# Splitting six output panels of a recurrent block ahead, and beginning them in six PSUM banks before its last channel tile is ready

## The reference

```python
def rglru_mixer(hx, hc, w_in, conv_w, conv_b, gate_w, gate_b, lam, w_out, need_ctx_out):
    ux = hx @ w_in
    gx, rx = ux[..., :D_RNN], ux[..., D_RNN:]            # D_RNN = 1280
    ...
    rx = centred_dwconv(rx, conv_w, conv_b)
    for d in range(2):                                   # two directions
        ax, bx = rglru_coeffs(rx, gate_w[d], gate_b[d], lam[d])
        ...                                              # h_x = linear_scan(ax, bx, h_c[:, -1])
    yx = (jax.nn.gelu(gx) * (hs_x[0] + hs_x[1]).astype(gx.dtype)) @ w_out
...
x = x + mx[:, :, 5] * yx
```

## Time and profile before

| | |
|---|---|
| median of 3 runs | 2760.24 us (2759.57 to 2760.76) |
| the profiled execution: its time, its span | 2758.28 us, 2756.5 us |
| PE, PEld busy | 2653.8 us (96%), 2476.4 us (90%) |
| DVE, ACT, POOL busy | 1428.3 us (52%), 763.1 us (28%), 895.8 us (32%) |
| DMA: moved, mean | 309.32 MB, 112 GB/s |
| granted PE clock over the span | 0.985 of full |

### The profile page before, as it was taken

How to read it: one execution, slowest core, us unless ns; L and a number is a source line. 1 busy time by engine, 2 the same in 40 slices (tenths; PEclk the granted TensorE clock), 3 DMA queues, 4 the chain that set the end, 5 groups by cost and what they waited for, 6 DMA issues and landing times.

```text
span 2756.5 us, 40602 instructions
## 1 busy us (share of the span) xinstructions
PE 2653.8 (96%) x15151; PEld 2476.4 (90%) x15151; DVE 1428.3 (52%) x2489; ACT 763.1 (28%) x1034; POOL 895.8 (32%) x418
## 2 busy tenths in 40 slices
PE   6999999999999899999999999999999997899998
PEld 5999999998968899999999899999998985778887
DVE  6666466565463666546666423422226995532233
ACT  4111122212164322111112322111114884332222
POOL 1332232322323232322222455545530002344442
PEclk9999999999999999999999999999999998999999
DMA  6443343423311243433442455545513442233332
GB/s 216 145 122 117 97 122 122 129 80 79 106 33 31 77 122 122 125 104 118 122 121 79 122 164 168 168 126 158 162 42 107 153 135 63 62 96 102 91 101 82
DMA packets 439330, 309.32 MB, mean 112 GB/s; under 512 B 9853, under 2 KB 414166, under 8 KB 439254
## 3 DMA queue, kind: packets, MB, share of 16 engines
q1 hardware_dynamic: 439254, 308.32, 36.7%
HBM read 278.92 MB, written 30.46 MB: 112 GB/s over the span
## 4 chain that ended last, share of the span: by engine, by line
PE 67%; issue 19%; POOL 6%; DVE 4%; DMA 2%; ACT 1%; SPq 1%; POOLq 0%; DVEq 0%; ACTq 0%
PE pair_a L1835 30%; PE pair_b L1835 29%; POOL w_lo L809 5%; DVE ada_sums L1258 1%; DMA unit_raw<-in_rg_gate_w_dram 1%; PE pair_b L1822 1%; PE pair_b L1823 1%; PE pair_b L1824 1%; DVE h_lo L1409 1%; PE pair_c L1924 1%; PE pair_a L1822 1%; POOL unit_hi L823 1%; PE pair_a L1823 1%; PE pair_a L1824 1%; DVE work_g L1398 0%
## 5 line engine op out<-in xcount | busy, mean ns | idle before, releaser
L809 POOL TENSOR_TENSOR w_lo<-raw,w_hi 128x1024 fp32r<-128x1024 f32 (+2 forms) x271 | 739.5, 2729 | 1652.4 <-ACT w_hi L932 1652.4
L932 ACT ACTIVATE w_hi<-raw 128x1024 fp32r<-128x1024 f32 (+2 forms) x271 | 308.9, 1140 | 1144.6 <-PE pair_b L1835 660.9
L1298 DVE TENSOR_TENSOR work_g<-work_s,pair_b 128x768 f32<-128x768 f32 (+1 forms) x88 | 78.1, 887 | 664.3 <-PE pair_b L1835 502.2
L1258 DVE SCALAR_TENSOR_TENSOR ada_sums<-ada_raw,cvec,ada_sums 128x256 f32<-128x256 f32 x896 | 388.5, 506 | 0.0
L1835 PE MATMUL pair_a<-h_hi,w_hi 128*128 128x384 f32 x1296 | 335.6, 339 | 6.4 <-POOL w_lo L809 3.9
L1835 PE MATMUL pair_a<-h_lo,w_hi 128*128 128x384 f32 x1296 | 331.0, 336 | 0.0
L1835 PE MATMUL pair_a<-h_hi,w_lo 128*128 128x384 f32 x1296 | 330.7, 336 | 0.0
L1835 PE MATMUL pair_b<-h_hi,w_hi 128*128 128x384 f32 x1168 | 296.7, 334 | 0.0
L1835 PE MATMUL pair_b<-h_hi,w_lo 128*128 128x384 f32 x1168 | 296.4, 334 | 0.0
L1835 PE MATMUL pair_b<-h_lo,w_hi 128*128 128x384 f32 x1168 | 296.2, 334 | 0.0
L1835 PEld LDWEIGHTS pair_a<-h_hi,w_hi 128*128 128x128 f32 x1296 | 232.8, 189 | 16.0 <-issue 9.9
(11 more groups left out here) (314 smaller groups left out, 4352.2 us busy)
## 6 DMA issues: line engine op xcount, KB each, us to landing
raw<-in_ffn_w_gu_dram SPq DMA_DIRECT2D x176, 512.0 KB, 3.9
ada_raw<-in_ada_w_dram SPq DMA_DIRECT2D x64, 1024.0 KB, 5.1
raw<-in_ffn_w_down_dram SPq DMA_DIRECT2D x64, 704.0 KB, 4.6
unit_raw<-in_rg_w_in_dram SPq DMA_DIRECT2D x40, 256.0 KB, 3.6
ada_first<-in_ada_w_dram SPq DMA_DIRECT2D x4, 2048.0 KB, 13.3
raw<-in_ab_w_in_dram SPq DMA_DIRECT2D x16, 512.0 KB, 3.9
u_split_dram<-unit_hi SPq DMA_DIRECT2D x20, 256.0 KB, 2.0
u_split_dram<-unit_lo SPq DMA_DIRECT2D x20, 256.0 KB, 2.3
```

The costliest lines, as they stand in the source:

```text
L809: nc.gpsimd.tensor_tensor(wl[:, par, 0:kt * P], raw[:, par, 0:kt * P], wh[:, par, 0:kt * P].bitcast(F32), ALU.subtract).then_inc(split_rea ...
L932: nc.scalar.activation(wh[:, par, 0:kt * P], raw[:, par, 0:kt * P], ACT.Copy).then_inc(hi_done, 1)
L1258: step = nc.vector.scalar_tensor_tensor(out=sums[v], in0=tiles(k), scalar=c_k, in1=sums[v], op0=ALU.mult, op1=ALU.add)
L1298: nc.vector.tensor_tensor(gbuf[:, 0, 0:W], sbuf[:, 0, 0:W], up, ALU.mult)\
```

## The change

- **Units.** 15 units more: `out_unit` splits the first 6 x 128 columns of `w_out` (`AHEAD` = 6) to a new HBM tensor `out_split`. Ten of them (4 panels wide, one k-tile) go one to each pair of `gu21`, which then has three units for a pair; five (2 panels wide, two k-tiles) go in `dn21`. The two gate units that were in `dn21` move to the first pair of `gu21`.
- **Buffers.** From unit 28 on there are two high buffers (`unit_hi` and `unit_hi2`), with a store counter for each side (`pair_stored`). SP issues a unit's load before it waits for the unit before it to be split and stored (`begin_unit`, `end_unit`, `step`, `units_of`).
- **Order in `dn20` and `dn21`.** Both panel loads and, in `dn20`, `load_ada` now go before the units; POOL does a panel's `low` before the unit, not after it.
- **Recurrent end.** SP loads the split panels from `out_split` (`load_out`): panel 0 and 1 to the two weight buffers, 2 to 5 to `out_hi`, `out_lo`, which lie over `h_hi`, `h_lo` and so wait for the last `g` product. PE does tiles 0 to 7 of panel 0 before the gates of tile 9, tiles 0 to 7 of panels 1 to 5 after them, each panel in a bank of its own (`OUT_BANKS`), then tile 8 of all six, then tile 9 of all six. Panels 6 and 7 are loaded early to `raw` and split by ACT and POOL once panels 0 and 1 are through. ACT's and POOL's splits of panels 0 to 5 go.

```diff
+        unit_hi2 = at("unit_hi2", [P, UNIT], F32R, scr_at + size([P, 4, T]) + size([P, T]))
+        out_hi = at("out_w_hi", [P, AHEAD - 2, KR * P], F32R, h_at)
+        out_lo = at("out_w_lo", [P, AHEAD - 2, KR * P], F32R, h_at + size([P, KD, T]))
...
+        OUT_BANKS = [pA[:, 0:512], pB[:, 0:512], pC[:, 0:512], pA[:, 512:1024], pB[:, 512:1024], pR[:, 0:512]]
...
+        UNITS_UP = [(28, 2)] + [(30 + 3 * i, 3) for i in range(KC - 1)]
+        UNITS_DOWN = [[(20 + 2 * i, 2) for i in range(4)], [(60, 2), (62, 2), (64, 1), (65, 0)]]
...
+            def begin_unit(k, r, src, later):
+                if isinstance(k, int) and k >= PAIRED + 2:
+                    sp.wait_ge(pair_stored[r], stored_before(k))
+                elif later or isinstance(k, int) and k >= PAIRED:
+                    sp.wait_ge(unit_stored, k * 32 - 31)
+                n = src.shape[-1]
+                sp.dma_start(unit_raw[r][:, :].rearrange("p (k n) -> p k n", n=n), src).then_inc(unit_landed[r], 16)
...
+            def step(k, unit):
+                begin_unit(k, k % 2, unit[0], True)
+                finish_held()
+                held.append((k, k % 2, unit[1]))
...
+                    def gate_up_ahead(i, k, units):
+                        for r in range(2):
+                            load(i * 2 + (split_no(p0) + r), r, KD, gu[:, :, span(i * P + (r * DFF + h * KC * P), P)])
+                            step(k + r, units[r])
+                        if len(units) > 2:
+                            step(k + 2, units[2])
...
-            sp.wait_ge(unit_stored, 50 * 32 + 1)
+            sp.wait_ge(unit_stored, PAIRED * 32 + 1)
+            for r in range(2):
+                sp.wait_ge(pair_stored[r], stored_before(60 + r))
...
+            for r in range(2):
+                p = P_RGOUT + AHEAD + r
+                load(split_no(p), r, KR, wro[:, :, (AHEAD + r) * P:(AHEAD + r + 1) * P])
+            for r in range(2):
+                sp.wait_ge(pair_stored[r], stored_before(66 - r))
+            sp.wait_ge(panel_used, u_panel(KR - 1) + 1)
+            load_out(0, 0, KR, out_landed[0])
             load_gates(KR - 1)
-            with sp.Fori(0, KD // 2) as i:
-                for r in range(2):
-                    load(i * 2 + (split_no(P_RGOUT) + r), r, KR, wro[:, :, span(i * (2 * P) + r * P, P)])
+            sp.wait_ge(panel_used, g_panel(KR - 1) + 1)
+            load_out(1, 0, KD, out_landed[1])
+            for n in range(2, AHEAD):
+                load_out(n, 0, KR, out_landed[n])
+            sp.wait_ge(panel_used, gate_panel(KR - 1) + 1)
+            load_out(1, KD, KR, out_end_landed)
...
+                    if P_RGOUT + AHEAD <= p < P_RGOUT + KD:
+                        act.wait_ge(panel_used, p - AHEAD + 1)
...
-                if n == KR - 1:
-                    high(P_RGOUT)
                 gelu_rows(n)
...
-            high(P_RGOUT + 1)
+            high(P_RGOUT + AHEAD)
+            high(P_RGOUT + AHEAD + 1)
             outputs("rgout", P_RGOUT)
...
-                    pe.wait_ge(resid_done, UPD[name] + KD - 2 + r - 1)
+                    pe.wait_ge(resid_done, UPD[name] + (KD - 2 + r - 1 if name != "rgout" else 4 + r))
...
+            pe.wait_ge(out_landed[0], 32)
+            pe.wait_ge(u_done, KR)
+            out_part(0, range(KR - 2))
             pe.wait_ge(gates_done, 4 * (KR - 1))
             gates((KR - 1) % 2, KR - 1)
+            for n in range(1, AHEAD):
+                pe.wait_ge(out_landed[n], 32)
+                if n == 1:
                     pe.wait_ge(gelu_x_done, KR)
                     pe.wait_ge(gelu_q, KR)
+                else:
+                    pe.wait_ge(gates_done, 4 * (KR - 1) + (2 if n == 2 else 4))
+                out_part(n, range(KR - 2))
+            pe.wait_ge(out_end_landed, 32)
+            for k in (KR - 2, KR - 1):
+                for n in range(AHEAD):
+                    last = out_part(n, [k])
+                    if k == KR - 1:
+                        last.then_inc(panel_used, 1)
+            tail("rgout", P_RGOUT, KR, yh, yl, None)
```

More of the change, by code:

```diff
@@ L219, in trunk @@
         gate_split = nc.dram_tensor("gate_split_dram", (KR, 2, P, 4 * P), F32, kind="Internal").ap()
+        out_split = nc.dram_tensor("rg_out_split_dram", (2, P, KR, AHEAD * P), F32, kind="Internal").ap()
         def alias(start, end):
@@ L316, in trunk @@
         gates_landed = sem("gates_landed")
+        out_landed = [sem(f"out_w_landed{n}") for n in range(AHEAD)]
+        pair_stored = [sem("unit_pair_stored0"), sem("unit_pair_stored1")]
+        out_end_landed = sem("out_w_end_landed")
         silu_done = sem("silu_done")
@@ L610, in gate_units @@
[L610 to L623, removed]
+            wro = rg_out[0].rearrange("(k p) n -> p k n", p=P)
@@ new lines, in _, with finish_held, units_of, side @@
+            held = []
+            def step(k, unit):
+                begin_unit(k, k % 2, unit[0], True)
+                finish_held()
+                held.append((k, k % 2, unit[1]))
+            def finish_held():
+                while held:
+                    end_unit(*held.pop())
+            def units_of(k, units):
+                def side(n):
+                    return (k + n) % 2 if isinstance(k, int) else n % 2
+                for n, (src, to) in enumerate(units):
+                    begin_unit(k + n, side(n), src, n >= 1)
+                    if n >= 1:
+                        end_unit(k + n - 1, side(n - 1), units[n - 1][1])
+                    yield
+                end_unit(k + len(units) - 1, side(len(units) - 1), units[-1][1])
@@ L833, in unit_pairs, with units_between @@
                         low(i * 2 + (p0 + r), r, kt)
+            def units_between(p0, kt, units):
+                for i, (k, n) in enumerate(units):
+                    for r in range(2):
+                        if kt == KC:
+                            low(i * 2 + (p0 + r), r, kt)
+                        if r < n:
+                            unit(k + r, (k + r) % 2)
+                        if kt != KC:
+                            low(i * 2 + (p0 + r), r, kt)
+                    if n > 2:
+                        unit(k + 2, k % 2)
             def split_ahead():
@@ L840, in split_ahead @@
                 unit_pairs(first["gu20"], 1, KC, KD, 0)
-                unit_pairs(first["dn20"], 0, KD // 2, KC, 20)
-                pairs(first["gu21"], 0, 1, KD)
-                unit_pairs(first["gu21"], 1, KC, KD, 28)
-                unit_pairs(first["dn21"], 0, 1, KC, 48)
-                pairs(first["dn21"], 1, KD // 2, KC)
+                units_between(first["dn20"], KC, UNITS_DOWN[0])
+                units_between(first["gu21"], KD, UNITS_UP)
+                units_between(first["dn21"], KC, UNITS_DOWN[1])
             def ffn(f):
```

147 lines of the change are left out of this document (86 added, 61 removed).

## The result

The changed kernel takes 2739.41 us (median of 4 runs, 2736.28 to 2740.07), the kernel before 2760.47 us beside it (4 runs): a ratio of 0.9924, 95% interval 0.9908 to 0.994, so 21.1 us faster where 26.0 were forecast. The time lies in the range of 2729 to 2743, between the forecast and the rival "`dn20` pays" (2738 to 2740). Two repeats later gave 2736.5 and 2738.6 us, 22.7 and 19.2 us under the kernel before in the same sets.

A forecast was written before the change was run, and what follows sets the result against it. PE, busy 96% of the span, was taken as the bound, with time won only in its waits and low clock. The recurrent end's 27.0 us less 1 for clock, others 0, gave 2760.2 - 26.0 = 2734.2 us; range 2729 to 2743.

The forecast's parts named there:

- `dn20` pays: Rival in `dn20`: held units delay panel loads, 3 to 6 us back, 2738 to 2740 us; chance 0.10.
- What bounded the end: Recurrent end: PE stands still or runs at low clock for 28.8 us of the 73.8 us before the tail.
- (a) to (c): Recurrent end: panel 0's eight tiles 5.45 us, gates 4.2, panels 1 to 5 27.3, last two tiles 8.2, without waits.
- The inputs: Recurrent end: the last y, ready at 2310.7 before, comes some 5 us earlier; tile 9 asks for it at 2313.3.
- The weights: Recurrent end: loads at 291 GB/s, panel 5 landing at 2296.5 and wanted at 2303.8; bound 10 us late.
- late weights: Rival at the recurrent end: `out_split` comes too slowly, up to 10 us given back, 2744 us; chance 0.07.
- (d): Start of the tail: panels 6 and 7 split after 0 and 1, ready at 2320.0, or 2322.7 if POOL goes on.
- (e): Tail: two half panels take 2 x 3.69 us without the 0.79 wait, to 2327.4 against 2354.38: 27.0 us.
- (f): Before the tail: PE stands 2.6 us, and the low clock after it costs 1 of 2 us.
- The end's sum: Recurrent end and tail: 27.0 us won, 1 us lost to the clock, sum 26.
- `gu21` and `dn21`: Ten more units in `gu21` (POOL 12.1 of a pair's 16.7 us, 47 GB/s on top of 147), five in `dn21`: cost 0.
- I take 0: `dn20`: earlier modulation tile could win 2.8 us, held units making panels late could lose 4 us; taken as 0.

The follow-up runs named there:

- `dn20` in its old order: Changed kernel with SP and POOL going over `dn20` as in the kernel before: 2734.34 us, ratio 0.9912.
- new order alone: Kernel before with only the changed kernel's `dn20` order (panel loads and modulation tile's load before units, POOL's low split before its unit): 2762.61 us, ratio 1.0009.
- by panel: Changed kernel, but each of the six panels does tile 8 and at once tile 9: 2733.25 us, ratio 0.9902.
- sums one panel earlier: Changed kernel, but in `dn20` DVE sums the next pair's modulation tile behind the even panel's update: 2731.85 us, ratio 0.9899.
- both: Changed kernel with the last two tiles panel by panel and `dn20`'s sums behind the even panel's update: 2732.99 us, ratio 0.9898.
- sums ahead of `gu20`: Kernel with both edits, plus `dn20`'s first modulation tile summed before `gu20` and the others loaded a pair earlier: 2732.57 us, ratio 0.9905.
- inside `gu20`: Kernel that sums `dn20`'s first modulation tile before `gu20`, but with these sums behind `gu20`'s second pair: 2728.44 us, ratio 0.9889.
- putting the gates first: Changed kernel, but PE does tiles 0 to 7 of panel 0 after the gates of tile 9: 2740.92 us, ratio 0.9932.

## Why the prediction came out as it did

The table gives the lengths on which it turns, in us. "End" is from the first product of panel 0 (before: from the end of the last `g` product) to the second token half.

| | `dn20` | end |
|---|---|---|
| before | 96.79 | 82.03 |
| changed, three profiles | 100.42, 98.83, 100.44 | 56.22, 56.21, 56.21 |
| `dn20` in its old order | 97.75 | 56.22 |
| new order alone | 100.44 | (old) |
| by panel; sums one panel earlier; both | 100.43; 98.06; 98.03 | 52.21; 56.20; 52.20 |
| sums ahead of `gu20`; inside `gu20` | 93.87; 93.87 | 52.21; 52.21 |

What PE lost in `dn20`, in us, read from its waits for the sums. The 1.6 us of low clock are the difference of the two changed profiles, whose waits are the same; the run with the sums one panel earlier shows the same fall of the clock (0.65 and 0.50 from 1724 to 1728). In each row the losses and the 93.87 of the last row make the length to 0.2 us.

| | first pair | pairs 2 to 4 | low clock | `dn20` |
|---|---|---|---|---|
| before | 1.57 | 1.25 | 0 | 96.79 |
| changed, first profile | 2.55 | 3 x 0.74 | 1.6 | 100.42 |
| changed, second profile | 2.54 | 3 x 0.74 | 0 | 98.83 |
| `dn20` in its old order | 0.94 | 1.26, 0.74, 0.74 | 0 | 97.75 |
| sums one panel earlier | 2.54 | 0 | 1.6 | 98.06 |
| sums inside `gu20` | 0 | 0 | 0 | 93.87 |

- **What bounded the end, right.** One reading was loose: the low clock did not last 3.5 to 5 us behind each of the four waits, since behind the one of 4.04 us only three matmuls follow (1.45 us). The sum does not use it.
- **(a) to (c), right.** 5.44, 4.17, 27.2 and 8.2 us, as computed, with no wait. That the convolution's wait could be filled was worth 7.4 us, shown by putting the gates first.
- **The inputs, right.** L1873 (L1778 before) took 0.95 to 0.97 us each time from 2284.44 on, and the last y was ready at 2311.25. With the end starting 5.7 us later in this execution, that is 5.2 us sooner; it is asked for at 2318.99.
- **The weights, right.** The queue moved 290 GB/s. It fell from 278 GB/s in 2301 to 2302 to 63 in the next microsecond, so panel 5 had landed by about 2302.5 (forecast: 2296.5, and 5.7 for the later start, 2302.2), and was wanted at 2309.5. The rival "late weights" had some 7 us to spare.
- **(d), right.** PE stood 2.28 us, 2.6 were forecast. DVE did get in between POOL's two splits (first the sum of squares at 2323.61, 1.10 us, then the update at 2324.63), and the next sum, with two SBUF inputs, was held (2.74 us).
- **(e) and (f), right in kind.** No wait inside the tail; the low clock behind the gap cost 1.6 us, 1 was forecast. The panel-by-panel order shows that both were avoidable.
- **The end's sum.** 25.8 us against this profile of before, 26.0 forecast. Against the second profile of the old end it is 23.5. The subtraction rested on one execution of a stretch with four low-clock spells, and its own scatter of 2.3 us was not in the forecast.
- **`gu21` and `dn21`, right.** POOL 133.7 us where 11 pairs of 12.1 make 133; 192 GB/s where 147 + 47 make 194; no microsecond lost.
- **`dn20`, wrong: the term "I take 0".** It costs 3.1 us on average (six profiles of this order at 98.8 or 100.4, mean 99.9, against 96.8). Neither end of the bound came true. The earlier tile was to end PE's wait for the sums, 2.8 us; the waits rose to 4.8. In the first pair the tile did come early, but POOL's second unit, now right behind the split, held DVE: 2.55 us in place of 1.57, and mostly the low clock behind it. In pairs 2 to 4 the sums ran beside POOL's split and unit (10.43 us, not 5.62), and the waits went from 1.25 to 2.2 us. The held unit was to make panel loads late; the panels land later, but PE never waited for `w_lo` there. The earlier trace rows showed the meeting from POOL's side, and the step asked only what POOL loses by it, not what DVE does.

That the time fell on the number of the rival "`dn20` pays" is luck as far as the mechanism goes: its 3 to 6 us were to come from late panel loads, and none was late.

What is shown of `dn20`, and what is not: that its new order costs the time (put back in one run, and alone in the kernel before in another), and that the waits for the sums with the clock behind them are all of the loss (93.87 us once they are gone). No run moves the tile's load without POOL's order, so their shares are read from the traces alone.

Together: -24.7 (the mean of the two subtractions at the end) + 3.1 = -21.6 us, beside the measured 21.1, 22.7 and 19.2.

The Trainium skill ("SBUF — State Buffer", section "SBUF: two separate sides") says that a two-input VectorE operation and a GpSimd operation exclude each other instruction by instruction. The 10.43 us agree with it in the main: beside 5.95 us of POOL's operations the sums lost 4.8. Its use in the prediction stopped at the end stage, though it bears on `dn20` as much.

Open stays why the wait of 2.54 or 2.55 us in `dn20` was followed by the low clock in four of the six profiles of the changed order and not in the two others; no run here changes what comes before it. The scatter of about 4 us in the unchanged first 1700 us was not studied either.

## What to carry to other kernels

- When a load is moved earlier, follow its consumer: it will start earlier too, and what it then runs beside decides. In the second pair the wait for the tile had kept the sums out of a collision.
- When the order on one engine changes, ask what its operations now stand beside on the others. Here POOL's unit moved behind its split and onto DVE's small operations ahead of the sums, and that pair lost the most.
- A series of short DVE operations with two SBUF inputs belongs where POOL is idle or where nobody waits. The first tile's 5.6 us of sums cost 0 inside `gu20` and 4.4 us ahead of it. The other three tiles' sums cost nothing in `dn20` when done early, though POOL meets them there too.
- When several panels share their last inputs, finish them one by one and not input by input: the first buffers come free earlier, and work that needs them hides behind the rest (4.0 us here).

## What the runs showed of the hardware

- POOL and DVE meeting do not share evenly, and who began first does not settle who waits. The 14 sums begun at 1739.62, 0.2 us after POOL's split, lost 4.8 us, and POOL's three operations took 5.95 us in place of the 5.55 that their usual 3.23, 1.04 and 1.28 us make. In the kernel before, 14 sums that had begun 2.0 us ahead of a unit kept their 5.62 us, and the unit's first operation took 4.49 instead of 1.04. But one pair later the sums had begun 1.4 us ahead of a unit, and it was they that lost 1.8 us, while POOL took 1.15 and 1.35 us:

```profile
1738.07 5.62 DVE L1258 SCALAR_TENSOR_TENSOR ada_sums<-ada_raw,cvec,ada_sums 128x256 f32<-128x256 f32 x14
...
1761.54 7.43 DVE L1258 SCALAR_TENSOR_TENSOR ada_sums<-ada_raw,cvec,ada_sums 128x256 f32<-128x256 f32 x14
```

```profile
1762.95 1.15 POOL L823 TENSOR_TENSOR unit_hi<-unit_raw,ones 128x512 fp32r<-128x512 f32 x1 [1.89 <-DMA unit_raw<-in_rg_gate_w_dram]
1764.17 1.35 POOL L825 TENSOR_TENSOR unit_lo<-unit_raw,unit_hi 128x512 fp32r<-128x512 f32 x1
```

In each of the three meetings one engine kept nearly its full pace and the other waited; what chooses between them is not shown.
- The gap of 2.28 us ahead of the tail was followed by the low clock, 1.6 us of it, in all six profiles that had it; the wait of 2.54 or 2.55 us in `dn20` only in six of eight, 1.6 us of it there as well.
